# A first Strassen pair whose sum of A12's product and first snapshot is formed early, with the next pair's snapshots and the conditioning row moved ahead

## What is computed

```python
x = x + 0.5 * g1 * swiglu(modulate(rmsnorm(x)), ffn_w1[0], ffn_w2[0])   # first feed-forward stage
x = x + g2 * hybrid_mixer(modulate(rmsnorm(x)))                         # gated mixing and a state-space scan
x = x + 0.5 * g3 * swiglu(modulate(rmsnorm(x)), ffn_w1[1], ffn_w2[1])   # second feed-forward stage

def swiglu(h, w1, w2):
    g, u = split(h @ w1, 2)          # 1024 -> 2 x 2816
    return (silu(g) * u) @ w2        # 2816 -> 1024
```

## Time and profile before

| | us |
|---|---|
| runs | median 1450.55 (1448.95 to 1452.12, 3 runs) |
| the profiled execution | 1447.58, of it the span from first to last instruction 1446.0 |
| TensorE matmuls busy | 1419.7 (98%) |
| TensorE weight loads busy | 1369.6 (95%) |
| VectorE busy | 1025.1 (71%) |
| ScalarE busy | 670.2 (46%) |
| TensorE's mean granted clock | 0.998 |

### The profile page before, as it was taken

How to read it: one execution, slowest core, us unless ns; L and a number is a source line. 1 busy time by engine, 2 the same in 40 slices (tenths; PEclk the granted TensorE clock), 3 DMA queues, 4 the chain that set the end, 5 groups by cost and what they waited for, 6 DMA issues and landing times.

```text
span 1446.0 us, 25675 instructions
## 1 busy us (share of the span) xinstructions
PE 1419.7 (98%) x10178; PEld 1369.6 (95%) x10178; DVE 1025.1 (71%) x1762; ACT 670.2 (46%) x1202; POOL 71.3 (5%) x121
## 2 busy tenths in 40 slices
PE   7999999999999999999999999999999999999998
PEld 6889999999999999998789999998999999999997
DVE  5777667676776776667876667557867676767776
ACT  5643525253435444666835453126525253444355
POOL 3100000000000130000100000003000000000001
PEclk9999999999999999999999999999999999999999
DMA  9752434445344612231352222443324223231221
GB/s 321 212 177 66 152 112 146 117 142 151 110 139 132 183 30 73 74 100 51 111 169 78 76 62 74 132 147 111 100 57 142 73 88 88 67 109 52 81 74 73
DMA packets 219565, 161.02 MB, mean 111 GB/s; under 512 B 6859, under 2 KB 204679, under 8 KB 219459
## 3 DMA queue, kind: packets, MB, share of 16 engines
q1 hardware_dynamic: 217490, 153.89, 35.8%
q0 software_dynamic: 1696, 5.56, 1.3%
q10 hardware_dynamic: 272, 0.10, 0.0%
HBM read 151.50 MB, written 8.03 MB: 110 GB/s over the span
## 4 chain that ended last, share of the span: by engine, by line
PE 91%; DVE 3%; ACT 1%; DMA 1%; POOL 1%; issue 1%; SPq 0%; DVEq 0%; ACTq 0%; POOLq 0%
PE acc L865 24%; PE acc L1208 19%; PE pC L1090 19%; PE acc L1090 14%; PE acc L1157 2%; PE acc L1076 2%; PE pB L987 2%; PE pC L1348 1%; DMA ada_raw<-in_w_ada 1%; PE pB L946 1%; PE pB L1333 1%; PE pC L1483 1%; PE pC L1367 1%; PE acc L882 0%; POOL hnf L788 0%
## 5 line engine op out<-in xcount | busy, mean ns | idle before, releaser
L1581 ACT ACTIVATE slot<-raw 128x512 fp32r<-128x512 f32 (+1 forms) x312 | 191.6, 616 | 236.7 <-PE acc L1208 137.8
L2176 DVE TENSOR_TENSOR slot<-raw,slot 128x512 fp32r<-128x512 f32 (+1 forms) x312 | 210.5, 676 | 53.0 <-ACT slot L1581 50.3
L1208 PE MATMUL acc<-hid_hi,slot 128*128 128x320 f32 x1240 | 238.6, 310 | 0.0
L1090 PE MATMUL pC<-hn_hi,slot 128*128 128x320 f32 x960 | 227.8, 310 | 0.0
L1208 PEld LDWEIGHTS acc<-hid_hi,slot 128*128 128x128 f32 x1240 | 195.1, 188 | 2.9 <-issue 2.1
L1090 PEld LDWEIGHTS pC<-hn_hi,slot 128*128 128x128 f32 x960 | 164.5, 188 | 2.9 <-issue 2.9
L865 PE MATMUL acc<-hn_hi,whi 128*128 128x320 f32 x672 | 161.1, 321 | 0.0
L1090 PE MATMUL acc<-tT,slot 128*128 128x320 f32 x960 | 155.0, 310 | 2.5 <-DVE tmp L2410 2.5
L865 PE MATMUL acc<-hn_hi,wlo 128*128 128x320 f32 x672 | 153.2, 309 | 0.0
L865 PE MATMUL acc<-hn_lo,whi 128*128 128x320 f32 x672 | 153.1, 309 | 0.0
L1090 PE MATMUL pC<-hn_lo,slot 128*128 128x320 f32 x480 | 148.3, 309 | 0.0
(11 more groups left out here) (389 smaller groups left out, 2367.9 us busy)
## 6 DMA issues: line engine op xcount, KB each, us to landing
raw<-in_ffn_w SPq DMA_DIRECT2D x86, 512.0 KB, 5.2
sraw<-in_w_ada SPq DMA_DIRECT2D x26, 1024.0 KB, 6.5
wraw<-in_w_in SPq DMA_DIRECT2D x36, 512.0 KB, 3.8
raw<-in_ffn_w SPq DMA_DIRECT2D x16, 1024.0 KB, 5.0
ada_raw<-in_w_ada SPq DMA_DIRECT2D x8, 1024.0 KB, 11.3
wraw<-in_w_out SPq DMA_DIRECT2D x16, 512.0 KB, 4.2
raw<-in_ffn_w SPq DMA_DIRECT2D x8, 768.0 KB, 4.4
sraw<-in_w_ada_final SPq DMA_DIRECT2D x6, 1024.0 KB, 7.4
```

Source lines behind the costliest of these rows:

```text
L1090: last = mm(out, w[:, kk * P:(kk + 1) * P], a, start=(first and kk == 0 and t == 0), stop=(kk == KQ - 1 and t == 2), skip_group_check=not ...
L1208: last = mm(a[h], w[t // 2][:, k, :], (hid_hi, hid_lo)[t % 2][:, k * TOK + h * HALF:k * TOK + (h + 1) * HALF], start=(k == 0 and t == 0), ...
L1581: A(slot_as(fi, b, 0), source_of(fi, b), ACT.Copy).then_inc(blk_hi, 1)
L2176: V.tensor_tensor(out=slot_as(fi, b, 1), in0=source_of(fi, b), in1=slot_as(fi, b, 0).bitcast(F32), op=ALU.subtract).then_inc(blk_lo, 1)
```

## The change

- VectorE forms c11 of pair 2 (`first_c11`) as soon as the w bank is finished, ahead of `hid_lo` of pair 1, in place of after c21 and c22.
- TensorE in pair 3 waits for two sums of pair 2 (c11 and c21) in place of three before it overwrites the z bank.
- ScalarE in pair 2: behind high half `b + 12` come the row copy (first stage only), then the snapshot s0 of pair 3, then the two Silus. High half `b + 13` and `hid_high` of pair 2 move into pair 3: high half `b + 13`, wait for all sums of pair 2, snapshot p7, `hid_high` of pair 2, snapshot s1, four high halves, snapshot s2.
- From pair 4 on nothing changes.

```diff
@@ TensorE, wino_pair
             else:
-                pe.wait_ge(c_sum, 3 * n)
+                pe.wait_ge(c_sum, 3 * n - int(p == PLAIN + 1))
             product(fi, b + 1, z_bank, t3, True)
@@ ScalarE, wino_pair
-            snapshot("s0", x, 1)
+            if p != PLAIN + 1:
+                snapshot("s0", x, 1)
...
+            elif p == PLAIN + 1:
+                blk(fi, b + 6)
+                act.wait_ge(c_sum, 3 * n)
+                snapshot("p7", z_bank, 2)
+                hid_high(fi, p - 1)
+                snapshot("s1", x, 3)
+                for j in range(7, 11):
+                    blk(fi, b + j)
+                snapshot("s2", x, 5)
             else:
...
             blk(fi, b + 11)
             blk(fi, b + 12)
-            act.wait_ge(c_sum, 3 * (n + 1))
+            if p == PLAIN:
+                if p in DUO_ROWS[fi]:
+                    duo_row(DUO_ROWS[fi][p])
+                act.wait_ge(c_sum, 3 * n + 1)
+                snapshot("s0", x_bank[(p + 1) % 2], SLOTS + 1)
+            else:
+                act.wait_ge(c_sum, 3 * (n + 1))
             A(silg[:, 0:HALF], c11, ACT.Silu)
             act.wait_ge(blk_done, fi * NB + b + 7)
             A(silg[:, HALF:TOK], x, ACT.Silu).then_inc(silu_done, 1)
-            blk(fi, b + 13)
-            hid_high(fi, p)
+            if p > PLAIN:
+                blk(fi, b + 13)
+                hid_high(fi, p)
@@ ScalarE, ffn
-                    if p in DUO_ROWS[fi]:
+                    if p in DUO_ROWS[fi] and p != PLAIN:
                         duo_row(DUO_ROWS[fi][p])
@@ VectorE
+        def first_c11(fi, p):
+            n = wino_before(fi, p)
+            dve.wait_ge(blk_done, fi * NB + BLK_PAIR[p] + 2)
+            dve.wait_ge(snap, 4 * n + 1)
+            dve.wait_ge(hidp_done, fi * N_PAIR + p)
+            V.tensor_tensor(out=c11, in0=snaps["s0"], in1=w_bank, op=ALU.add).then_inc(c_sum, 1)
@@ VectorE, wino_pair
                 blk(fi, b + 5)
+                first_c11(fi, p)
                 hid_low(fi, p - 1)
...
             if p > PLAIN:
                 dve.wait_ge(blk_done, fi * NB + b + 6)
-            dve.wait_ge(hidp_done, fi * N_PAIR + p)
-            V.tensor_tensor(out=c11, in0=snaps["s0"], in1=w_bank, op=ALU.add).then_inc(c_sum, 1)
+                dve.wait_ge(hidp_done, fi * N_PAIR + p)
+                V.tensor_tensor(out=c11, in0=snaps["s0"], in1=w_bank, op=ALU.add).then_inc(c_sum, 1)
             blk(fi, b + 12)
             first_sums(fi, b + 14)
             dve.wait_ge(silu_done, fi * N_PAIR + p + 1)
-            dve.wait_ge(c_sum, 3 * n + 2)
+            dve.wait_ge(c_sum, 3 * n + 2 + int(p == PLAIN))
```

## The result

The changed kernel takes 1440.28 us (median of 4 runs, 1440.15 to 1442.02), the kernel before 1450.68 us in the same comparison: 10.4 us less, a ratio of 0.9932 with a 95% interval of 0.9914 to 0.9949. The profiled execution took 1440.15 us with a span of 1438.4, 7.6 us shorter than the span of before. The timed gain is thus 2.8 us larger than what the two traces show, and that difference is the main thing the experiments are about.

The account below looks back on a forecast made before the run. TensorE's matmuls cover 1419.7 of 1446.0 us, so only its standstill or slow running can be won: 3.72 + 2.67 + 1.02 + 0.78 = 8.19 us, 1450.55 - 8.2 = 1442.4. The forecast covers 1441 to 1443.8, with most of two rivals 1439.5 to 1445.8.

Parts of the forecast that it names:

- the two waits: TensorE's waits in pair 3: 3.5 us for ScalarE's `srow` in the first stage, 2.5 us for c11 in the second.
- First stage: Pair 3's second product takes over at 86.42 instead of 82.70, held by the late row copy: 3.72 us to gain.
- (a): Second stage, pair 3's second product: waiting for c11, it starts at 1035.59 instead of 1032.92, 2.67 us lost.
- (b): Second stage, pair 3's third product: snapshot s0, late behind Silus and `hid_hi`, costs 1.02 us that the page hides.
- (c): Second stage, pair 3's third product: the clock's lower level after the 2.5 us stall costs 0.78 us.
- The reserves of 0.5, 0.3 and 0.4 us: Second stage after the change: time by which snapshots s0, p7 and s1 end before TensorE needs them, so no stall.
- The load of the down projection: SyncE's second load, late for ScalarE after the change, hidden by other down products: price nothing, at most 1 to 2 us.
- A wait for `hid_lo` in the first down product: Sign in the changed profile, at the down projection after pair 3, that would show the prediction wrong.
- rival 1: The clock fell behind both stages' stalls in most timed runs: 1.7 us more, gain 9.9, time 1440.6 us; 20%.
- Level changes from run to run: Skill's rule: clock may fall behind either stall, both or none, so the gain lies between 7.4 and some 9.9 us.
- The wait passing on to a snapshot: Rival, second stage: s0, p7 and s1 come late one after another; gain 5.4 us, time 1445.2 us; 12%.
- The clock staying low through pair 3: Rival, both stages: three short waits keep the clock low, 24.6 us of slow matmuls, time 1470 us; 2%.

Follow-up runs that it names:

- row_only: The kernel before with only the first stage's row copy moved ahead of ScalarE's wait for the sums: 1445.91 us, ratio 0.9973.
- sum_only: The kernel before with only the VectorE and TensorE part (c11 early, two sums awaited), ScalarE's queue unchanged: 1449.06 us against 1450.57.
- three_sums: The changed kernel with TensorE waiting for all three sums of pair 2 again: 1443.14 us against 1440.49.
- fill: The kernel before with idle products of constants put into TensorE's two stalls to keep the clock up: 1447.02 us, ratio 0.9977.
- load_later: The changed kernel with the 2 MB conditioning load issued behind the second down projection load: 1440.87 us, repeated at 1440.83.
- s0_only: The whole change in the first feed-forward stage alone, second stage as in the kernel before: 1445.1 us against 1449.67.
- s1_only: The whole change in the second feed-forward stage alone, first stage as in the kernel before: 1445.37 us, ratio 0.997.
- look_before: The kernel before, unchanged, run once more for a second trace: 1449.42 us, span 1447.8.
- before: The kernel before the change, in its first profiled execution: 1447.58 us, span 1446.0.
- s0_late: The changed kernel with pair 3's snapshot s0 put back behind pair 2's Silus, the high half and `hid_hi`: 1445.65 us against 1440.49.
- again: The changed kernel, unchanged, timed once more beside other experiments: 1440.49 us, ratio 0.9935.

## Why the prediction was right, and where it was off

**What bounds, and where the time was lost.** Right: the two waits are gone and nothing else in pair 3 of either stage took their place; behind it the new 0.4 us is the only loss (waits in the start-up and the loads for the conditioning vary by some tenths from run to run). The queue of ScalarE as the cause of the first is shown by `row_only`: the copy alone turns 3.51 us of waiting into 0.56 + 0.75.

**First stage.** Forecast 3.72 us. At the third product the lead is 3.75 us (88.03 less 84.28). The order of row copy, s0, Silus, p7, `hid_hi`, s1 ran within 0.1 us of the forecast times, or a little ahead of them, as the durations laid end to end are an upper bound.

**Second stage, three parts.** (a) 2.67 us: shown by `sum_only`, in which the wait for c11 is gone and passes to s0, and by `three_sums`, in which the same product waits 1.52 us again. (b) 1.02 us that the page did not show: shown by `fill`, where it appears in full. (c) 0.78 us for the clock, in truth nearer 0.67: from the start of the second product to the end of the third it took 1041.07 - 1035.59 = 5.48 us before, and 1040.55 - 1035.74 = 4.81 in `fill` at full clock. The forecast set the third product at 1.92 us, but one that starts behind a wait takes 2.03, and the 0.11 belongs to the wait. The sum of the three stands. At the end of the third product of pair 3 the changed kernel is 7.5 us ahead; 3.0 of this it had at the end of pair 3's first product, so 4.5, as forecast (4.47). The reserves of 0.5, 0.3 and 0.4 us turned out at 0.6, 0.8 and 0.6.

**The load of the down projection.** Here a step failed, though it cost little. I took the end of the traffic (90.8 us) for the landing of the load, and then held 4.4 us of down products for more than enough cover. The load was issued earlier by 0.35 us but landed at 92.7, 7.5 us after its issue, behind the 2 MB of the conditioning weights; the traffic's share was 0.71 in the microsecond from 90 and still 0.22 in the one behind it. The trace of before had the landing too: issued at 85.52, the view of DMA issues for that load gives 7.2 us from issue to landing, so 92.7 where the forecast took 90.8. After the change ScalarE stood 2.55 us for its block and not 1.2. The chain behind it took 5.1 us (92.73 to 97.83), so the cover was short by 0.4 us. `load_later` shows the cause: with the load ahead of the 2 MB the wait is gone. A wait for `hid_lo` in the first down product was one of the signs that the prediction named for being wrong, and it came, at 0.4 us and not at 1 to 2.

**The sum.** Forecast 8.2 us, measured 10.4. The waits were right; the term that was mis-sized is the clock's. I put it at the 0.78 us of the one trace and gave the case that it falls behind both stalls 20%, on the ground of 1.00 in the one execution seen. `fill` measures 3.3 us for the clock in both stages by the means. By stage, `s0_only` leaves 5.6 - 3.3 = 2.3 us for it in the first and `s1_only` 4.8 - 3.7 = 1.1 in the second, each good to about a microsecond. Single traces show 1.3 us (`look_before`: transposes and second product 3.50 us from 86.49 to 89.99, against 2.20) and 2.4 us (`s1_only`) lost in the first stage.

The measured 1440.28 lies below the forecast's own 1441 to 1443.8, in the part of the range that was there for rival 1; that rival's time, 1440.6, is the one that came. Its size is in part luck, as its 1.7 us for the first stage leaves out the new 0.4 and the average is nearer 2.3. The hint was in the numbers: the profiled execution of before was 3 us faster than the median of its own runs, and I carried that distance over as a constant, whereas it was a part of what the change would remove. After the change the profiled execution and the median are 0.1 us apart, and the runs spread over 1.9 us instead of 3 to 6.

One end stays open. Runs of the kernel before at a clock of 0.993 must hold some (0.998 - 0.993) x 1450 / 0.5 = 14.5 us more of the lower level than the profiled one (an estimate from the granted clocks of the runs), and the longest that a trace shows in the first stage is 6.8. No trace is of such a run, so how its low time is shared out between the stages is not known; that filling the two stalls removes it is.

**Level changes from run to run.** Three executions with the same stall of 3.51 us (`before`, `look_before`, `s1_only`) lost 0, 1.3 and 2.4 us behind it. The Trainium skill, TensorE: Matmul & The Clock Gate, section "What's actually happening", has one program change level at other points from run to run; the traces agree. The sum by that rule reached to 9.9 us, nearer to the 10.4 measured than the sum by the single trace.

**Rivals.** The wait passing on to a snapshot did not happen in the changed kernel, but `sum_only` shows that it does if the snapshots stay where they were. The clock staying low through pair 3 (slower) did not happen.

## What to carry to other kernels

Where an engine's queue is written by hand, a short copy that another engine waits for belongs ahead of the long waits of its queue: 0.37 us of work moved past one wait gained 4.2 us by itself, and the snapshot s0 put back behind its old place cost 5.0. Freeing one wait behind another pays only when the next one in the same queue moves too, so follow the queue until the last consumer has cover. When the profiled execution is faster than the median of its kernel's runs, ask what it happened to be spared; stalls near which the clock may fall cost more on average than one trace shows.

## What the runs showed of the hardware that was not expected

The clock fell to its lower level with no wait of TensorE listed: in both traces of `load_later` at about 615.2 us, behind eight microseconds of transposes and narrow products (clock 0.91 on average from 600 to 620, 1.6 us lost), and in `s0_late` at 616.7. In the three traces of the changed kernel the same work comes 0.4 to 0.7 us later than in `load_later`, and the clock stayed at 1.00; in `s0_late` it comes 1.1 us later, and the clock fell. So the shift does not explain the fall, and the higher group of `again` suggests that it comes without one too. A gain of half a microsecond is smaller than what such a fall takes or leaves.

Behind the same stall of 3.51 us the low level lasted from not at all up to 6.8 us, from 84.8 (while TensorE still stood) to 91.6, with 0.50 in each full microsecond between, as the stretches of `s1_only` show at both ends:

```profile
84.00:85.00 1.00, 0.00 (x0) 0.00 (x0) 0.74 (x2) 0.85 (x3) 0.00 (x0) 0.88 1.09 376
...
90.00:91.00 1.00, 1.00 (x5) 1.00 (x5) 0.00 (x0) 0.79 (x2) 0.00 (x0) 0.50 1.01 365
91.00:92.00 1.00, 1.00 (x6) 1.00 (x6) 0.80 (x2) 0.17 (x1) 0.00 (x0) 0.71 0.10 27
```
